# Prompt attention on one Trainium2 core: bias by matmul, one minimum pass, exponential from PSUM, 64-row scores

## The reference, cut to what matters

```python
def diff_attention(q, k, v, q_pos, k_pos, lam):
    B, Tk = k.shape[:2]
    k = k.reshape(B, Tk, DA_HEADS, 2, DA_HEAD_DIM)
    s = jnp.einsum('bqhmd,bkhmd->bhmqk', q, k, preferred_element_type=jnp.float32) * (DA_HEAD_DIM ** -0.5)
    dist = jnp.abs(q_pos[:, None] - k_pos[None, :]).astype(jnp.float32)
    bias = -alibi_slopes()[:, None, None] * dist
    causal = k_pos[None, :] <= q_pos[:, None]
    s = jnp.where(causal, s + bias[:, None], -jnp.inf)
    p = jax.nn.softmax(s, axis=-1)
    a = p[:, :, 0] - lam * p[:, :, 1]
    return jnp.einsum('bhqk,bkhd->bqhd', a, v)

def diff_post(o, subln_g, lam_init):
    B, T = o.shape[:2]
    return (rms_norm(o) * subln_g * (1.0 - lam_init)).reshape(B, T, DA_WIDTH)
```

## Time and profile before

| what | value |
|---|---|
| median of 3 runs | 1923.88 us (1921.61 to 1924.16) |
| the profiled execution: its own time | 1933.34 us |
| the profiled execution: its span | 1931.1 us |
| mean granted TensorE clock | 0.961 of full |
| busy: TensorE, VectorE, ScalarE, GpSimd | 1796.5, 780.2, 668.2, 85.3 us |
| DMA | 203.84 MB, mean 106 GB/s |

### The profile page before, as it was taken

How to read it: one execution, slowest core, us unless ns; L and a number is a source line. 1 busy time by engine, 2 the same in 40 slices (tenths; PEclk the granted TensorE clock), 3 DMA queues, 4 the chain that set the end, 5 groups by cost and what they waited for, 6 DMA issues and landing times.

```text
span 1931.1 us, 32720 instructions
## 1 busy us (share of the span) xinstructions
PE 1796.5 (93%) x13119; PEld 1687.8 (87%) x13119; DVE 780.2 (40%) x1082; ACT 668.2 (35%) x899; POOL 85.3 (4%) x113
## 2 busy tenths in 40 slices
PE   5999999998998776999979999899999899999996
PEld 5999999987997545888869999669998799999996
DVE  2333332234323775777753223244344433333123
ACT  3333331124223555677743222123322433332111
POOL 0000000000001420000000000210000000000002
PEclk9999999998998997999989999889999999999998
DMA  4222223231431015788742232242222122222221
GB/s 140 87 87 87 87 87 98 82 94 38 134 113 44 1 30 174 268 275 300 269 131 66 77 109 66 75 154 88 87 88 87 35 88 89 88 88 84 85 98 46
DMA packets 146665, 203.84 MB, mean 106 GB/s; under 512 B 5538, under 2 KB 127330, under 8 KB 146594
## 3 DMA queue, kind: packets, MB, share of 16 engines
q1 hardware_dynamic: 145442, 198.35, 31.6%
q0 software_dynamic: 1152, 4.46, 0.6%
HBM read 191.39 MB, written 11.40 MB: 105 GB/s over the span
## 4 chain that ended last, share of the span: by engine, by line
PE 86%; DVE 5%; ACT 4%; issue 3%; DMA 0%; SPq 0%; POOL 0%; POOLq 0%; DVEq 0%; ACTq 0%
PE ps L295 68%; PE ps L1187 3%; PE ps L1208 2%; PE ps L1230 2%; PE ps L972 1%; PE ps L986 1%; PE ps L1635 1%; PE ps L1627 1%; PE ps L612 1%; PE ps L1246 1%; DVE vp_lo L1325 1%; DVE kt_lo L1304 1%; PE ps L697 1%; ACT vp_hi L1321 1%; ACT aT L1067 1%
## 5 line engine op out<-in xcount | busy, mean ns | idle before, releaser
L295 PE MATMUL ps<-xh,w_hi_t 128*128 128x272 f32 x2432 | 510.0, 291 | 25.6 <-DVE xl L649 18.2
L295 PE MATMUL ps<-xh,w_lo_t 128*128 128x272 f32 x2432 | 505.3, 289 | 0.0
L295 PE MATMUL ps<-xl,w_hi_t 128*128 128x272 f32 x2432 | 504.1, 289 | 0.0
L281 DVE TENSOR_TENSOR w_lo_t<-w_raw,w_hi_t 128x2048 fp32r<-128x2048 f32 (+1 forms) x112 | 252.4, 2254 | 519.2 <-ACT w_hi_t L277 519.2
L295 PEld LDWEIGHTS ps<-xh,w_hi_t 128*128 128x128 f32 x2432 | 384.5, 190 | 30.4 <-issue 21.1
L295 PEld LDWEIGHTS ps<-xl,w_hi_t 128*128 128x128 f32 x2432 | 385.0, 190 | 0.0
L295 PEld LDWEIGHTS ps<-xh,w_lo_t 128*128 128x128 f32 x2432 | 382.2, 190 | 0.0
L277 ACT CAST w_hi_t<-w_raw 128x2048 fp32r<-128x2048 f32 (+1 forms) x112 | 209.9, 1874 | 277.2 <-PE ps L295 277.2
L295 PE MATMUL ps<-hh,w_lo_t 128*128 128x272 f32 x704 | 145.7, 288 | 0.0
L295 PE MATMUL ps<-hh,w_hi_t 128*128 128x272 f32 x704 | 145.5, 288 | 0.0
L295 PE MATMUL ps<-hl,w_hi_t 128*128 128x272 f32 x704 | 145.1, 288 | 0.0
(11 more groups left out here) (241 smaller groups left out, 2069.7 us busy)
## 6 DMA issues: line engine op xcount, KB each, us to landing
w_raw<-in_ffn_w_gu_dram SPq DMA_DIRECT2D x44, 1024.0 KB, 5.0
w_raw<-in_w_in_dram SPq DMA_DIRECT2D x32, 1024.0 KB, 5.7
k_page<-in_cache_k_dram SPq DMA_DIRECT2D x64, 512.0 KB, 4.7
v_page<-in_cache_v_dram SPq DMA_DIRECT2D x64, 512.0 KB, 4.4
w_raw<-in_ffn_w_down_dram SPq DMA_DIRECT2D x16, 1024.0 KB, 5.1
w_raw<-in_ffn_w_down_dram SPq DMA_DIRECT2D x8, 768.0 KB, 4.6
w_raw<-in_w_branch_a_dram SPq DMA_DIRECT2D x4, 1024.0 KB, 5.0
st_in<-in_state_ret_dram SPq DMA_DIRECT2D x8, 512.0 KB, 5.0
```

The source lines that it names most:

```text
L281: nc.vector.tensor_tensor(w_lo_t[:, j, 0:nk], w_raw[:, j, 0:nk], w_hi_t[:, j, 0:nk].bitcast(F32), ALU.subtract).then_inc(lo_split, 1)
L295: mm = nc.tensor.matmul(ps[:, bank + half, 0:HALF], w[:, j, k, w_cols], m[:, k0 + k, half * HALF:half * HALF + HALF], start=start and k == ...
```

## The change

- The bias is added by TensorE: per unit and map an fp32r matmul of `slope_ident` (the identity times minus the head's slope) with `dist_r` opens the accumulation, and the scores are added to it. ScalarE prepares both tiles once, between the projections of values and queries (`act_seeds`). The query projection scales by -1/8, so PSUM holds minus the scaled and biased scores.
- Each map's scores use that map's own 64 rows of `qaT` and `kaT`; `q_stage`, `bias8`, `s_sb` and GpSimd's work for them go.
- VectorE takes both maps' minimum in one reduction (`low`). ScalarE's exponential reads PSUM.
- The combination is (p1 times ratio) minus p0 in one pass, with ratio = lambda sum0 / sum1. The sign goes with the copy of `aT`, and 1 / sum0 with the copy of the output (`keep_output`), which so waits for the reciprocal.
- TensorE's order becomes scores of u + 2, transposes of u, values of u - 1, and all units are written out, with no loops.
- The head norm's squares of the first three blocks are made by GpSimd during the attention, and their sums by VectorE behind the units 11, 19 and 27. The square root's table is loaded ahead of the last output copy. SyncE loads `bias_stage`, which lies where the squares lie, only when the last sum is made.
- The decode's queries take the factor -8 back when they are split. Two small constants, `slope8` and `map_rows`, are no longer loaded, and `START_LOADS` is 9.

The core of the diff; lines that are only removed are left out below `low`.

```diff
-        s_sb = at("s_sb", A + 71680, [2, 2, 512])
+        sq_att = at("sq_att", A + 71680, [2, D])
...
-        bias8 = at("bias8", M, [2, 512])
-        q_stage = at("q_stage", M + 4096, [2, 2, P])
+        slope_ident = at("slope_ident", M, [HA, P], F32R)
+        dist_r = at("dist_r", M + 4096, [SEQ], F32R)
...
+        class AttentionNorm(HeadNorm):
+
+
+            def pool_squares(self, pool):
+                for b, (src, _, r) in enumerate(self.blocks[:-1]):
+                    pool.wait_ge(attn.o_set, HA * (b + 1) + 2)
+                    pool.wait_ge(self.summed, self.b0 + b + 1)
+                    nc.gpsimd.tensor_tensor(self.squares[0:r, b % 2], src, src, ALU.mult).then_inc(self.sq_done, 1)
+
+            def act_squares(self, act):
+                b = len(self.blocks) - 1
+                src, _, r = self.blocks[b]
+                act.wait_ge(self.summed, self.b0 + b + 1)
+                act.wait_ge(attn.o_set, HA * NB + 2)
+                nc.scalar.activation(self.squares[0:r, b % 2], src, ACT.Square).then_inc(self.sq_done, 1)
+                act.wait_ge(self.guarded, self.p0 + 1)
+                nc.scalar.activation(ssd[:, self.parts[0][1]], ss[:, self.parts[0][1]], ACT.Sqrt).then_inc(self.sd, 1)
+
+            def dve_sums(self, dve, b):
+                g, n = self.g, self.n
+                r = self.blocks[b][2]
+                dve.wait_ge(self.sq_done, self.b0 + b + 1)
+                nc.vector.tensor_reduce(ss[0:r, b * g:b * g + g],
+                                        self.squares[0:r, b % 2].rearrange("p (h d) -> p h d", d=n), AX_X, ALU.add
+                                        ).then_inc(self.summed, 1)
+
+            def dve_scale(self, dve):
+                self.dve_sums(dve, len(self.blocks) - 1)
+                self.dve_rows(dve)
...
+            def act_seeds(self, act):
+                act.wait_ge(att_const, 16)
+                nc.scalar.copy(dist_r[:], dist[:]).then_inc(self.seeds, 1)
+                for h in range(HA):
+                    nc.scalar.mul(slope_ident[:, h], ident[:], -(2.0 ** -(1.0 + h))).then_inc(self.seeds, 1)
+            def scores(self, pe, u):
+                i, h, s, n = self.where(u)
+                pe.wait_ge(self.exped, u + 1)
                 for m in range(2):
-                    mm = nc.tensor.matmul(ps[:, 2 * s + m, 0:n], q_stage[:, s, m], kaT[:, h, 0:n], start=True, stop=True)
+                    nc.tensor.matmul(ps[:, 2 * s + m, 0:n], slope_ident[:, h], dist_r[:, SEQ - n:SEQ], start=True, stop=False)
+                for m in range(2):
+                    rows = slice(DH * m, DH * m + DH)
+                    mm = nc.tensor.matmul(ps[:, 2 * s + m, 0:n], qaT[rows, h, P * i:P * i + P], kaT[rows, h, 0:n],
+                                          start=False, stop=True)
                 mm.then_inc(self.scored, 1)
...
             def pe_part(self, pe):
-                def head(h):
-                    return bass.ds(h, 1)
-                self.scores(pe, 0, head(0), 0, 0)
-                self.scores(pe, 0, head(1), 1, 1)
-                for i in range(NB):
-                    u0 = HA * i
-                    with pe.Fori(0, HA // 2 - 1) as hp:
-                        for s in range(2):
-                            self.scores(pe, i, head(2 * hp + s + 2), s, u0 + 2 * hp + s + 2)
-                            self.turn(pe, i, s, u0 + 2 * hp + s)
-                            self.values(pe, i, 2 * hp + s, s, u0 + 2 * hp + s)
-                    for s in range(2):
-                        if i + 1 < NB:
-                            self.scores(pe, i + 1, head(s), s, u0 + HA + s)
-                        self.turn(pe, i, s, u0 + HA - 2 + s)
-                        self.values(pe, i, HA - 2 + s, s, u0 + HA - 2 + s)
-            def scale(self, dve, i, s, u):
-                n = self.keys(i)
+                pe.wait_ge(self.seeds, HA + 1)
+                self.scores(pe, 0)
+                self.scores(pe, 1)
+                for u in range(self.UNITS):
+                    if u + 2 < self.UNITS:
+                        self.scores(pe, u + 2)
+                    self.turn(pe, u)
+                    if u:
+                        self.values(pe, u - 1)
+                self.values(pe, self.UNITS - 1)
...
+            def low(self, dve, u):
+                i, h, s, n = self.where(u)
                 dve.wait_ge(self.scored, u + 3)
                 dve.wait_ge(self.exped, u + 1)
                 nc.vector.memset(rsum[:, 2 * s:2 * s + 2], 0.0)
+                nc.vector.tensor_reduce(nmax[:, 2 * s:2 * s + 2], ps[:, 2 * s:2 * s + 2, 0:n], AX_X, ALU.min
+                                        ).then_inc(self.lowest, 1)
+            def combine(self, dve, u):
+                i, h, s, n = self.where(u)
+                r = 2 * (u % 4)
                 dve.wait_ge(self.exped, u + 3)
+                if u >= 4:
+                    dve.wait_ge(self.o_set, u - 1)
+                nc.vector.reciprocal(rr[:, r:r + 2], rsum[:, 2 * s:2 * s + 2]).then_inc(self.recip, 1)
                 dve.wait_ge(self.recip, u + 1)
+                nc.vector.scalar_tensor_tensor(ratio[:, s:s + 1], rsum[:, 2 * s:2 * s + 1], lamv[:, 1:2], rr[:, r + 1:r + 2],
+                                               ALU.mult, ALU.mult).then_inc(self.ratio_set, 1)
+                dve.wait_ge(self.ratio_set, u + 1)
                 dve.wait_ge(self.turned, u + 1)
+                nc.vector.scalar_tensor_tensor(a_sb[:, s, 0:n], p_sb[:, s, 1, 0:n], ratio[:, s:s + 1],
+                                               p_sb[:, s, 0, 0:n], ALU.mult, ALU.subtract).then_inc(self.combined, 1)
+            def dve_part(self, dve, norm):
+                self.low(dve, 0)
+                for u in range(self.UNITS):
+                    if u + 1 < self.UNITS:
+                        self.low(dve, u + 1)
+                    self.combine(dve, u)
+                    if u >= HA and u % HA == 3:
+                        norm.dve_sums(dve, u // HA - 1)
...
+            def exp(self, act, u):
+                i, h, s, n = self.where(u)
+                act.wait_ge(self.lowest, u + 1)
                 act.wait_ge(self.combined, u + 1)
                 for m in range(2):
                     k = slice(2 * s + m, 2 * s + m + 1)
+                    ins = nc.scalar.activation(p_sb[:, s, m, 0:n], ps[:, 2 * s + m, 0:n], ACT.Exp, bias=nmax[:, k],
                                                scale=-1.0, accum_out=rsum[:, k])
                 ins.then_inc(self.exped, 1)
+            def keep_turned(self, act, u):
+                i, h, s, n = self.where(u)
                 act.wait_ge(self.turned, u + 3)
                 act.wait_ge(self.pv, u + 1)
+                nc.scalar.mul(aT[:, s, 0:n], ps[:, 4 + s, 0:n], -1.0).then_inc(self.aT_set, 1)
+            def keep_output(self, act, u):
+                i, h, s, n = self.where(u)
                 act.wait_ge(self.pv, u + 3)
+                act.wait_ge(self.recip, u + 1)
+                nc.scalar.mul(o_nat[:, i, h * DV:h * DV + DV], ps[:, 6 + s, 0:DV], self.first_sum(u)).then_inc(self.o_set, 1)
             def act_part(self, act):
+                self.exp(act, 0)
+                for u in range(self.UNITS):
+                    if u + 1 < self.UNITS:
+                        self.exp(act, u + 1)
+                    self.keep_turned(act, u)
+                    if u:
+                        self.keep_output(act, u - 1)
+                nc.scalar.activation(sd[:, 0:1], guard[:], ACT.Sqrt)
+                self.keep_output(act, self.UNITS - 1)
...
-                nc.scalar.copy(qs_hi[:], qaT[:, :, SEQ:T]).then_inc(self.qk_hi, 1)
+                nc.scalar.mul(qs_hi[:], qaT[:, :, SEQ:T], -DH ** 0.5).then_inc(self.qk_hi, 1)
...
-        pq = Project(C_QA, 4, direct=qaT)
+        pq = Project(C_QA, 4, direct=qaT, scale=-DH ** -0.5)
...
-        START_LOADS = 11
+        START_LOADS = 9
...
-            const_load(sp, slope8[:], "slope8", const_landed)
-            const_load(sp, map_rows[:], "map_rows", const_landed)
...
-            sp.wait_ge(attn.combined, HA * NB + 2)
+            sp.wait_ge(HeadNorm.summed, NB + 2)
             const_load(sp, bias_stage[0:ROWS], "bias_dec", dec_const, ROWS)
...
             pv.act_part(act)
+            attn.act_seeds(act)
             pq.act_part(act)
...
-            pool.wait_ge(att_const, 16)
-            attn.pool_part(pool)
+            attn_norm.pool_squares(pool)
```

More of the change, by code:

```diff
@@ L246, in build @@
         rsum = tiny("rsum", 4)
-        rr = tiny("rr", 4)
+        rr = tiny("rr", 8)
+        ratio = tiny("ratio", 2)
         ss = bn[:, 0:32]
@@ L960, in pool_part @@
-            def pool_part(self, pool):
-                for i in range(NB):
-                    with pool.Fori(0, HA // 2) as hp:
-                        for s in range(2):
-                            self.pool_unit(pool, i, bass.ds(2 * hp + s, 1), s, HA * i + 2 * hp + s)
-            def scores(self, pe, i, h, s, u):
-                n = self.keys(i)
```

(21 more changed lines are left out.)

97 lines of the change are left out of this document (13 added, 84 removed).

## The result

| | before | after |
|---|---|---|
| median, us | 1923.88 (1921.61 to 1924.16) | 1894.37 (1893.94 to 1896.82) |
| ratio to before, 95% interval | | 0.9854 (0.9842 to 0.9867) |
| the profiled execution: its own time, its span | 1933.34, 1931.1 | 1896.65, 1894.8 |
| mean granted TensorE clock | 0.961 | 0.962 |
| busy: TensorE, VectorE, ScalarE, GpSimd | 1796.5, 780.2, 668.2, 85.3 | 1783.0, 754.2, 669.1, 47.7 |

The changed kernel is 29.5 us faster. Forecast were 18 us and 1906, with an own range of 1900 to 1911; the result lies 5.6 us under that, and just under the low end, 1895, of the wider range.

The account below looks back on a forecast made before the run. TensorE was taken to bound the changed attention, its own sum being the unit's period. Savings of 13.9 (attention), 0.4 (its start), 2.3 (tail) and 1.3 (front) sum to 17.9 us: median 1906, own range 1900 to 1911, wider 1895 to 1919.

Parts of the forecast that it names:

- the aT wait: Attention units: TensorE's wait for ScalarE's copy of aT, 0.9 us at 512 keys, would be covered by the new order.
- TensorE's own sum: Attention units: TensorE's steps added up would be the period, 3.75 us at 512 keys and 2.20 at 256.
- the two switches: Attention units: going to 64-row scores and back costs TensorE 0.35 us per unit, 0.4 at 1.2 GHz.
- 13.9 saved: Whole attention, first to last value step: 85.0 us against 98.9 before.
- all four as two: Scores at 512 keys: four instructions in the time of two, excluded because one map's two share their rows; three, 1.30, taken.
- the ring of 2.0: Units of 128 and 256 keys: with free switches, the ring with seeds and latencies would bound at 2.0 us.
- The tail: Last value step to the decode's first key copy: 17.9 us against 20.2, 2.3 saved.
- the added wait: Tail: the decode bias issues behind the last sum, signs land late, VectorE stands 3 us; 2.3 saved of 4.3 offered.
- The front: Kernel start: two small constant loads fewer let TensorE begin earlier, 1.3 us saved; ends 0 and 1.6.
- Scores in a row: Rival, attention: the maps' scores don't overlap, +0.43 us per unit at 512 keys, 8 in all, 1914; chance 0.28.
- Switches free: Rival, attention: the drain of mode switches lies under the fp32 streams, 11 us less, 1896; chance 0.08.
- TensorE stays at 1.2 GHz: Rival, attention: half-array scores may keep the clock at 0.50, through 384 keys 1939; chance 0.08, one-block lag (1919) 0.04.

Follow-up runs that it names:

- e3: The changed kernel with the values back in their old place, behind the transposes of their own unit: 1927.55 us, ratio to before 1.0034.
- e4: The changed kernel without the bias seeds, so no bias and no causal mask in the scores: 1887.2 us (one run).
- e1: The changed kernel with both maps' scores over all 128 rows of the head: 1903.59 us, ratio to before 0.9899.
- e2: The changed kernel with both maps' scores on the same 64 rows: 1938.57 us, ratio to before 1.0089.
- e7: The changed kernel with the norm's squares at another address, so the decode bias loads ahead of the attention's end: 1892.12 us, ratio to before 0.9841.
- e5: The changed kernel with two small constant loads put back at the start of SyncE's list: 1896.49 us (one run).
- e10: The kernel with both maps' scores on the same 64 rows, plus 24 products of no use before the first values: 1906.28 us, ratio to before 0.9906.
- e9: The changed kernel with 24 products of no use in TensorE's gap before the first values: 1893.12 us, ratio to before 0.9842.
- e12: The changed kernel with moved squares, 24 products of no use before the first values and 6 behind the last: 1890.33 us, ratio to before 0.9822.
- e6: The changed kernel with SyncE loading key pages and signs ahead of the sums and the decode bias behind them: 1898.66 us, ratio to before 0.9887.

## Why the prediction was right, and what was mis-sized

**What was right.** Faster, and why: the aT wait went (e3), TensorE's own sum became the period at 512 keys, at 128 and in most of the block of 384, with VectorE and ScalarE beside it, the seeds cost 0.46 for 0.50 (e4), the two switches 0.34 for 0.35 (e1 with e2), and no new wait took back the gain. At 256 keys the ring over VectorE set the period (below), which the sum of TensorE's steps doesn't have.

**What was mis-sized** is the attention's sum, "13.9 saved" where the trace shows 27.7, or 85.0 us forecast and 70.8 taken. The 24 units up to 384 keys were put at 58.2 us, with 4.0 beside them for low clock, norm sums and block changes, and took 51.4 with all of these; the five full units of 512 keys took 14.8 for 18.8, the last two 4.6 for 4.0. Two terms of the full-clock unit were mis-sized. At 512 keys:

| us | forecast | measured | from |
|---|---|---|---|
| seeds | 0.50 | 0.47 | chain after |
| scores and switch | 1.30 + 0.35 | 1.06 | chain after |
| transposes | 0.45 | 0.59 | chain after |
| values | 1.15 | 0.89 | chain after |
| unit | 3.75 | 3.01 | |

(In the chain half of the switching sits in the steps beside the scores, so e1 and e2 are the cleaner split: 0.88 and 0.34.) The scores carry most of it: with 0.88 for four at 512 keys in place of 1.30, and as much in proportion below, the forecast would by my estimate have been about 8 us lower. I excluded "all four as two", because the two instructions of one map share their rows. That reason held for one map's pair and didn't bear on two maps: the first instruction of each goes beside the other's, then the second ones, and the condition on rows is met each time. The program has one product per map, one behind the other, and the starts after show just that, two at 674.62 and two at 675.15. The Trainium skill, TensorE: Matmul & The Clock Gate, Part 3, says that products on distinct row groups run concurrently; the measured 0.88 for four fp32 instructions agrees, and e2's 1.91 shows that the rows are the condition. The Trainium skill, TensorEngine Tiling (Array Packing), section Tiling Modes, says that a change of mode drains TensorE; the 0.34 us per unit for two changes are in line with that, and didn't outweigh the gain.

The values were a smaller miss: 1.15 was the length of that step in a ring in which TensorE waited before it. In a stream without gaps it is 0.89, and e3 brings the 1.16 back. A duration read beside a wait holds part of the wait.

At 384 keys the chain has 0.35, 0.85, 0.48 and 0.67 for the same four steps, 2.35 us for a forecast 2.97; the eight take 2.49 each, since the last three already issue the scores of 512 keys and one (2.75) waits for VectorE's norm sum. At 256 keys eight units took 15.88, 1.98 each for 2.20. TensorE's own steps add up to 1.69 there, as in every other unit, and in between it waits for VectorE's combination:

```profile
642.13 0.44 PE L1010 MATMUL ps<-ident,a_sb 128*128 128x128 f32 x2 [0.60 <-DVE a_sb L1055]
```

The chain of this block goes over VectorE's steps and the waits between them. So "its own sum is the period" doesn't hold at 256 keys, and the ring of 2.0 that I named under the free switches was reached. At 128 keys it was 1.89 at half clock for 2.1.

**The tail.** 19.1 us from the last value step, 17.9 forecast. The mechanism is the forecast one, and its steps came nearly to the tenth: the signs issued 6.5 us behind the bias, landed 4.87 later, and VectorE stood waiting for them, 3.29 us for 3. Off are the end of the sum (4.7 for 4.4) and the last stretch from the signs to the key copy (2.9 for 2.2), in which the key copy waits 0.73 us for products at half clock (eight take 1.94 us, in e7 1.07). The gain was 1.1 for 2.3 by this count. I let the added wait take 2.0 of the 4.3 that the shorter norm offers; e7, where that wait is gone, has 3.5 less behind the last transposes.

**The front.** 1.3 forecast. TensorE's first instruction came 1.02 us earlier, and at the last query eviction 0.2 was left. Both lie within what executions of kernels with the same nine loads differ by (1.16 and 2.3 us, see e5), so the term is neither confirmed nor refuted; nothing shows a gain. The start of the attention gained 0.7 us for 0.4.

**The rivals.** *Scores in a row* has fallen: the starts exclude it. (It is the first rival; where the forecast calls it the second, the count is off.) *Switches free*, at 1896, is nearest to the result by its number, and its reason is wrong: the switches are paid, and the scores were cheaper than I allowed. *TensorE stays at 1.2 GHz* didn't happen in the changed kernel (1.00 from about 633 us), yet it was a real danger: e2 and e3 kept 0.50 until 675 and 653 us and were slower than before. The mechanism that I gave it, half the rows in use, is neither shown nor excluded: e10 shows that such units don't bring the clock down, not that they don't hold it down. That the range missed by 0.6 us comes mostly from a case that I excluded by a reason instead of by a row.

**What stays open:** what lets the clock rise again, within units that keep TensorE busy, at 621 us in one kernel and 675 in another, and whether the rows in use have a part in it; what e3 would take at full clock; and which later part of the kernel e9's runs differ in.

## What to carry to other kernels

Look at the order of the work on the engine that bounds before the length of its steps: moving one stage behind the next unit's was worth 0.95 us here, in a unit that then took 3.0. Two fp32 products over 64 rows each belong on different halves of the array and next to each other: here that was worth 0.85 us a unit, for 0.34 of switches. Where TensorE's clock fell in a gap, what was lost was not the gap but the half-speed stretch behind it, 4.7 us here and 24 in e2, so look in front of a dense stretch; and give a scratch buffer an address of its own before making a transfer wait for it.

## What was not expected of the hardware

- Four fp32 score instructions of 512 columns on two halves of the rows take 0.88 us, the same four on one half 1.73.
- In the gap before the third unit's seeds, 5.7 us in the changed kernel, the clock fell to 0.50, and it stayed there for 7 us (614.2 to 621.1, e1) to 61 us (613.6 to 675.0, e2), although TensorE was busy again from about 617 on. With 24 products in the gap it was at 1.00 throughout the attention in the profiled executions of all four kernels that have them (e9 to e12).
- The last small load of the start, issued at 7.8 to 7.9 us, let TensorE begin at 12.47 us in one execution (after) and at 13.24 in another (e6): 0.8 us of difference without any in the issue.
